# A fused block and two hybrid layers on one core: scaling of h spread later, h turned by VectorE and DRAM, V projected 512 columns at a time

## The reference

```
def hybrid_layer(x, norm_gain, w_in, w_out, rel_bias, cos, sin):
    hn = rms_norm_2(x, norm_gain)
    proj = hn @ w_in.astype(hn.dtype)
    cuts = list(np.cumsum(SPLIT_WIDTHS)[:-1])          
    aq, ak, av, ag, rq, rk, rv, rg = jnp.split(proj, cuts, axis=-1)
    ya = chunked_rel_attention(aq, ak, av, rel_bias)
    yr = chunkwise_retention(rq, rk, rv, cos, sin)
    y = jnp.concatenate([ya * jax.nn.silu(ag), yr * jax.nn.silu(rg)], axis=-1)
    return x + y @ w_out

def second_block(x, positions, norm_gain, w_in, w_out, rel_bias, final_gain):
    cos, sin = rotary_tables(positions, RET_HEAD_DIM)
    for layer in range(2):
        x = hybrid_layer(x, norm_gain[layer], w_in[layer], w_out[layer], rel_bias[layer], cos, sin)
    return rms_norm_2(x, final_gain)
```

## Time and profile before

| what | value |
|---|---|
| median of three runs | 1208.0 us (1207.38 to 1208.96) |
| profiled execution: time, span | 1208.31 us, 1206.5 us |
| TensorE (PE) busy, share of the span | 1192.2 us, 99% |
| VectorE (DVE) | 863.5 us, 72% |
| ScalarE (ACT) | 586.3 us, 49% |
| GpSimd (POOL) | 280.9 us, 23% |
| mean granted TensorE clock | 0.994 of full |

### The profile page before, as it was taken

One profiled execution on the slowest core, in us unless ns is written; L12 is line 12 of the kernel. 1 busy time (PEld: TensorE's weight loads), 2 busy tenths in 40 slices (PEclk: granted clock), 3 DMA queues, 4 the chain that ended last, 5 costly groups with the idle time before them and its releaser, 6 DMA issues.

```text
span 1206.5 us, 15740 instructions
## 1 busy us (share of the span) xinstructions
PE 1192.2 (99%) x5901; PEld 1012.0 (84%) x5901; DVE 863.5 (72%) x1425; ACT 586.3 (49%) x1048; POOL 280.9 (23%) x299
## 2 busy tenths in 40 slices
PE   8999999999999999999999989999999999999998
PEld 7888888888888888888888879899888889899886
DVE  6789655556786578537776798887747788986746
ACT  6666432324343344324435576854445577764442
...
GB/s 188 137 71 70 97 88 101 92 101 91 132 83 69 137 105 89 69 128 99 99 93 93 100 183 168 197 169 70 76 66 107 99 217 200 177 138 70 77 71 70
DMA packets 207697, 135.33 MB, mean 112 GB/s; under 512 B 5418, under 2 KB 200452, under 8 KB 207492
## 3 DMA queue, kind: packets, MB, share of 16 engines
...
## 4 chain that ended last, share of the span: by engine, by line
PE 93%; DVE 3%; ACT 1%; issue 1%; DMA 1%; SPq 0%; DVEq 0%; ACTq 0%
PE ps L191 92%; PE ps L194 1%; DVE b_sets L164 1%; DVE wlo L164 1%; DMA xtm<-in_x_dram 1%; ACT whi L161 0%; DMA raw<-in_w_in_dram 0%; ACT b_p L161 0%; DVE tmp L164 0%; DVE xtm L178 0%; ACT x1l L161 0%; DVE b_p L178 0%; SPq L197 0%; DVE b_pd L182 0%; ACT h L161 0%
## 5 line engine op out<-in xcount | busy, mean ns | idle before, releaser
L161 ACT ACTIVATE whi<-raw 128x1024 fp32r<-128x1024 f32 (+1 forms) x198 | 206.6, 1051 | 305.3 <-PE ps L191 294.5
L164 DVE TENSOR_TENSOR wlo<-raw,whi 128x1024 fp32r<-128x1024 f32 (+1 forms) x192 | 245.0, 1282 | 48.8 <-ACT whi L161 48.2
L191 PE MATMUL ps<-x0h,whi 128*128 128x512 f32 x1008 | 256.1, 392 | 0.0
L191 PE MATMUL ps<-x0l,whi 128*128 128x512 f32 x1008 | 255.5, 392 | 0.0
L191 PE MATMUL ps<-x0h,wlo 128*128 128x512 f32 x1008 | 254.0, 390 | 0.0
L191 PEld LDWEIGHTS ps<-x0h,wlo 128*128 128x128 f32 x1008 | 188.3, 188 | 38.8
L191 PEld LDWEIGHTS ps<-x0h,whi 128*128 128x128 f32 x1008 | 188.4, 189 | 38.2
L191 PEld LDWEIGHTS ps<-x0l,whi 128*128 128x128 f32 x1008 | 187.5, 188 | 38.0
L164 POOL TENSOR_TENSOR sums<-sums,sq 128x512 f32<-128x512 f32 x28 | 43.6, 1568 | 423.3 <-ACT sq L161 423.3
L191 PE MATMUL ps<-x1h,wlo 128*128 128x512 f32 x304 | 82.3, 389 | 0.0
L191 PE MATMUL ps<-x1h,whi 128*128 128x512 f32 x304 | 82.3, 389 | 0.0
(11 more groups left out here) (191 smaller groups left out, 1694.8 us busy)
## 6 DMA issues: line engine op xcount, KB each, us to landing
raw<-in_w_in_dram SPq DMA_DIRECT2D x98, 512.0 KB, 4.1
raw<-in_w_up_dram SPq DMA_DIRECT2D x44, 512.0 KB, 3.8
raw<-in_w_out_dram SPq DMA_DIRECT2D x24, 512.0 KB, 4.1
...
raw<-in_w_down_dram SPq DMA_DIRECT2D x16, 512.0 KB, 4.1
...
```

The lines of the kernel that those rows point to most:

```text
L161: return AC.put(lambda e: e.activation(o, i, func, **kw), after, AC, 1)
L164: return on.put(lambda e: e.tensor_tensor(o, a, b, op), after, on, 1)
L191: return PE.put(lambda e: e.matmul(o, l, r, start=start, stop=stop), after, PE if mark else None, 1)
```

## The change

The scaling of `H` in the first layer is taken out of `norm_steps` and becomes eight `h_final(k)`, begun at steps 49, 52, ... 70 of `layer_b(0)`, still on POOL. `h_turn(k)` no longer uses TensorE: VectorE turns the 32x32 blocks of a piece into `b_pd`, a DMA writes them to DRAM, and four `h_back(i)` DMAs read them back into `H`, tokens on the partitions, in another order of the columns, which the last additions follow through views of 32 columns. `project_v` is called twice a layer: 512 columns of V, 96 matmuls of 512 columns into four banks, one hook for each, weight tiles of two k by 512 columns, split one by one. The order of the projections, the steps of the heads and of the retention, and the inside of `ret` change with it: the third score comes one step earlier, the split takes two pieces instead of three and ends a step earlier, and `rsqrt_of` is on VectorE instead of POOL.

```diff
-            order = [4, 0, "v", 12, 5, 1, 13, 6, 2, "v", 14, 7, 3, 15]
-            order += [20, 16, "v", 21, 17, "v", 22, 18, 28, 23, 19, 29, 30, 31]
-            v_cols = iter([1024, 1280, 3072, 3328])
+            order = [4, 0, 5, "v", 1, 12, 6, 2, 13, 7, 3, 14, 15]
+            order += [20, 16, 21, "v", 17, 22, 18, 28, 23, 19, 29, 30, 31]
+            v_cols = iter([1024, 3072])
             for m in order:
                 if m == "v":
                     c0 = next(v_cols)
-                    plan_tm(wi2, 0, c0, 4, 256)
-                    plan_tm(wi2, 4, c0, 4, 256)
+                    for k0 in range(0, 8, 2):
+                        plan_tm(wi2, k0, c0, 2, 512)
...
-                    t2 = spread(RB2[:, :], r[:, 0:16], t)
-                    for k in range(8):
-                        t = tt(Hk(k), Hk(k), RB2[:, :], ALU.mult, after=[t2, h_read[k]], on=PO)
-                        h_tok[k] = ts(Hk(k), Hk(k), FIN(k), None, ALU.mult, after=t, on=PO)
-                    rb2_free.append(t)
+                    rb["rb2"] = spread(RB2[:, :], r[:, 0:16], t)
...
+        turn_free, h_back_tok = [[], []], []
+        HT = nc.dram_tensor("h_turned", (1024, 512), F32).ap()
...
-                ws, bs = [W.take() for _ in range(2)], [banks.next() for _ in range(2)]
-                free = [[], (), [v_read.get(s) for s in (0, 1)], [q_read.get(s) for s in (2, 3)]][j]
+                bs = [banks.next(), banks.next(), 5 + j, banks.next()]
+                frees = [[], []] if j == 0 else [[v_read[s] for s in (0, 1)], [q_read[s] for s in (2, 3)]]
                 r, tr_ = st["r"]
...
+                def evac(t, tok):
+
+                    bank, parts = bs[t], []
+                    for half in range(2):
+                        v = v_at(2 * j + half, t)
+                        if j == 0:
                             v = v.rearrange("p s (e c) -> p (s e) c", c=128)
-                        parts.append((v[:, :, 0:n], v[:, :, n:2 * n], src.rearrange("p (h c) -> p h c", c=n), r[:, t:t + 1]))
-                    for hi, _, src, rt in parts:
-                        th = act(hi, src, scale=rt, after=[tok, tr_, free])
+                        src = PS[bank][:, 256 * half:256 * half + 256].rearrange("p (h c) -> p h c", c=n)
+                        parts.append((half, v[:, :, 0:n], v[:, :, n:2 * n], src))
+                    th = [act(hi, src, scale=r[:, t:t + 1], after=[tok, tr_, frees[half]]) for half, hi, _, src in parts]
                     yield 1
...
+                    tl = [stt(lo, src, r[:, t:t + 1], f32(hi), ALU.mult, ALU.subtract, after=[tok, tr_, th, frees[half]])
+                          for half, hi, lo, src in parts]
                     bank_free[bank] = [th, tl]
...
+                    for half in range(2):
+                        tok_v.setdefault(2 * j + half, []).extend([th[half], tl[half]])
+
+                for kb in range(4):
+                    i, wh, wl = W.take()
+                    for t in range(4):
+                        for kk in range(2):
+                            k = 2 * kb + kk
+                            xh, xl = (x[:, k, 128 * t:128 * t + 128] for x in (X0.hi, X0.lo))
+                            first, end = k == 0, k == 7
+                            mm(PS[bs[t]][:, :], xh, wh[:, kk, :], first, False,
+                               after=[X0.th[k], W.hi[i], claim(bs[t]) if first else ()])
+                            hook()
+                            mm(PS[bs[t]][:, :], xh, wl[:, kk, :], False, False, after=[W.lo[i]])
+                            hook()
+                            tok = mm(PS[bs[t]][:, :], xl, wh[:, kk, :], False, end, after=[X0.tl[k]],
+                                     mark=end or (kk == 1 and t == 3))
+                            hook()
+                        if kb == 3:
+                            begin(evac(t, tok))
+                    W.done[i] = tok
+                    begin(W.split())
...
+            def h_final(k):
+
+                t = tt(Hk(k), Hk(k), RB2[:, :], ALU.mult, after=[rb["rb2"], h_read[k]], on=PO)
+                h_tok[k] = ts(Hk(k), Hk(k), FIN(k), None, ALU.mult, after=t, on=PO)
+                slot_free[5].append(t)
+                yield
+
...
+                o2, tp2 = score(2, 5, 0, claim(5))
                 yield 1
                 kp, pb, pfree = rps.take()
                 t0 = decay(0, o0, tp0)
...
                 t1 = decay(1, o1, tp3)
                 t3 = decay(3, o3, tp3)
                 bank_free[4] = [t3]
-                o2, tp2 = score(2, 5, 0, claim(5))
+                t2 = decay(2, o2, tp2)
+                bank_free[5] = [t2]
                 yield 1
                 _, pt, tfree = ptbs.take()
                 hi, lo = pt[:, 0:1280], pt[:, 1280:2560]
-                t2 = decay(2, o2, tp2)
-                bank_free[5] = [t2]
-                th = [act(hi[:, 0:512], pb[:, 0:512], after=[t0, tfree]),
-                      act(hi[:, 512:1024], pb[:, 512:1024], after=[t3, tfree])]
-                yield 1
-                th.append(act(hi[:, 1024:1280], pb[:, 1024:1280], after=[t2, tfree]))
+                cuts = ((0, 512), (512, 1280))
+                th = [act(hi[:, a:b], pb[:, a:b], after=[(t0, t2)[j], tfree]) for j, (a, b) in enumerate(cuts)]
+                yield 1
                 tl = [tt(lo[:, a:b], pb[:, a:b], f32(hi[:, a:b]), ALU.subtract, after=[th[j], tfree])
-                      for j, (a, b) in enumerate(((0, 512), (512, 1024)))]
-                yield 1
-                tl.append(tt(lo[:, 1024:1280], pb[:, 1024:1280], f32(hi[:, 1024:1280]), ALU.subtract, after=[th[2], tfree]))
+                      for j, (a, b) in enumerate(cuts)]
...
-                rr, t4 = rsqrt_of(sc, 4, 1.0 / 128, 1e-6, t3, on=PO)
+                rr, t4 = rsqrt_of(sc, 4, 1.0 / 128, 1e-6, t3)
...
-                free = claim(6)
-                for t in range(4):
-                    tp = tr(PS[6][:, 128 * t:128 * t + 128], H[:, 512 * k + 128 * t:512 * k + 128 * t + 128], IDENT,
-                            after=[h_tok[k], free], mark=t == 3)
-                yield 1
-                h_tok[k] = act(Hk(k), PS[6][:, :], after=[tp, h_read[k]])
-                bank_free[6] = [h_tok[k]]
-
+                pd = PD[:, 512 * (k % 2):512 * (k % 2) + 512]
+                t = blocks(pd.rearrange("p (i t c) -> p i t c", i=4, t=4),
+                           Hk(k).rearrange("p (t i c) -> p i t c", t=4, i=4), after=[h_tok[k], pd_free[0], turn_free[k % 2]])
+                turn_free[k % 2] = [dma(HT[128 * k:128 * k + 128, :], pd, d_ht[k % 2], after=t)]
+                h_read[k].append(t)
+                yield
+
+            def h_back(i):
+
+                src = HT.rearrange("(x j) (i c) -> i j x c", x=32, i=4)[i]
+                h_back_tok.append(dma(H[32 * i:32 * i + 32, :].rearrange("p (x c) -> p x c", c=128), src, d_hb,
+                                      after=[turn_free, [h_read[k] for k in range(8)]]))
+                yield
 
             start = step_no[0]
             at_step = lambda n, work: agenda.setdefault(start + n, []).append(work)
-            at_step(13 - l, head(0, 1))
-            for i in range(1, 8):
-                at_step(13 - l + 6 * i if i == 0 else 12 + 6 * i, head(i))
-            evs = []
-            for s in range(4):
-                evs += [ev_k(s), ev_q(s)] + [s // 2] * (s % 2 == 0) + [ev_g(s)]
-            for s in range(4, 8):
-                evs += [ev_r(s, "kh", "kl", rk_tok), ev_r(s, "qh", "ql", rq_tok)]
-                evs += [[2], [3], [ev_g(4)], [ev_g(5), ev_g(6), ev_g(7)]][s - 4]
-            for i, n in enumerate((66, 74, 82, 91)):
+            for i, n in enumerate((13 - l, 20, 27, 32, 37, 42, 48, 54)):
+                at_step(n, head(i))
+            att = [(ev_k, 0), (ev_q, 0), (ev_k, 1), 0, (ev_q, 1), (ev_g, 0), (ev_k, 2), (ev_q, 2), (ev_g, 1), (ev_k, 3), (ev_q, 3),
+                   (ev_g, 2), (ev_g, 3)]
+            rk = lambda s: ev_r(s, "kh", "kl", rk_tok)
+            rq = lambda s: ev_r(s, "qh", "ql", rq_tok)
+            att += [(rk, 4), (rq, 4), (rk, 5), 1, (rq, 5), (rk, 6), (rq, 6), (ev_g, 4), (rk, 7), (rq, 7), (ev_g, 5), (ev_g, 6),
+                    (ev_g, 7)]
+            evs = [e if isinstance(e, int) else e[0](e[1]) for e in att]
+            for i, n in enumerate((67, 76, 84, 92)):
                 at_step(n - 1, a_step_later(ret(i)))
-            if l == 1:
-                for k, n in enumerate((64, 66, 68, 74, 76, 78, 80, 85)):
-                    at_step(n, h_turn(k))
+            if l == 0:
+                for k in range(8):
+                    at_step(49 + 3 * k, h_final(k))
+            else:
+                for k in range(8):
+                    at_step(63 + 2 * k, h_turn(k))
+                for i in range(4):
+                    at_step(81 + 2 * i, h_back(i))
...
-        hv = H[:, :].rearrange("p (k t c) -> p k t c", k=8, c=128)
+        hv = H[:, :].rearrange("p (x t c) -> p x t c", t=4, c=32)
```

(1 more changed line is left out.)

43 lines of the change are left out of this document (7 added, 36 removed).

## The result

| | before | changed |
|---|---|---|
| median | 1208.0 us | 1214.96 us (1211.8 to 1215.6, five runs) |
| ratio | | 1.0052, 95% interval 1.0038 to 1.0065 |
| profiled execution: span | 1206.5 us | 1212.4 us |
| mean granted clock | 0.994 | 0.994 |

The account below looks back on a forecast made before the run. TensorE, busy 99% of the span, was taken as the bound. Terms -15.1 + 2.7 + 1.5 + 4.0 = -6.9 us gave 1201.4 us profiled, 1201.0 as median; range 1195 to 1207.

Parts of the forecast that it names:

- the waits that had a price in the forecast (8.2): New TensorE waits at bank 2 in layer 0's V, `ret(0)`'s V products and `ret(1)`'s scores: +2.7, +1.5 and +4.0 us.
- -5.0 (V): V projection: 384 matmuls of 512 columns replace pairs of 256 columns, saving 13 ns each, -5.0 us.
- -3.5 (turns): Turns of `H`: eight sets of four transposes leave TensorE, -3.5 us; their replacement costs nothing except in chains.
- Bank 2 in the first V call: TensorE waits for VectorE's evacuation of `ev_k(1)` to free the fourth bank: +2.7 us in layer 0, nothing in layer 1.
- a rival with 20%: The clock falls once or twice at a new wait, 3.0 us each: 1204 to 1207 us; chance 20%.
- `ret(1)`'s scores: At step 76 TensorE waits for the chain ending in VectorE's low part: +1.7 us in layer 0, +2.3 in layer 1.
- `ret(0)`'s V: Products with V wait behind VectorE's tiles and `b_pt`'s low part: 0.4 us in layer 0, 1.1 in layer 1, +1.5 together.
- The step that failed: Other moved heads finding `b_sets` or `b_pt` late was left uncosted, with slack claimed over 2 us in row order.
- the changed inside of `ret`: The rest of `ret`, two pieces instead of three and one step earlier, moves only low parts with slack; no cost.
- The -6.6: At `head(2)` of `layer_b(0)`, spreading the scaling of `H` removes the 3.6 us wait and 3.0 us of lower clock: -6.6 us.
- The rival on the slower side: Lower clock follows three of four new waits, 3.0 us each, and the waits stay: +2.1 us, 1210.1 and up; chance 8%.

Follow-up runs that it names:

- f5: Changed kernel with all but V's part undone, except that `ret` keeps its earlier third score and two pieces: 1210.93 us, ratio 1.0024.
- f2: Kernel before with only the turns of `H` moved to VectorE and DRAM: 1204.52 us, ratio 0.9972.
- g1: Changed kernel with bank 7 in place of bank 2 as fourth bank of each layer's first V call: 1209.56 us, ratio 1.0013.
- e3: Changed kernel with the eleven small `stat` rows of the retention norm on POOL again: 1211.06 us, ratio 1.0027.
- f1: Kernel before with only the scaling of `H` moved to steps 49 to 70: 1203.55 us, ratio 0.9963.
- e1: Changed kernel with the scaling of `H` back at the start of the first layer: 1211.88 us, ratio 1.0033.
- e2: Changed kernel with seven of the eight pieces of `H` left unscaled in the first layer: 1211.17 us, ratio 1.0030.
- f3: Changed kernel without its V part (V in quarters of 256 columns, with the order and heads' steps of before): 1200.95 us, ratio 0.9942.
- g5: Changed kernel with banks 7 and 5 as V's fourth, `head(6)`'s and `ret(1)`'s products with V one step later, norm's small rows on POOL: 1199.90 us.

## Why the prediction was wrong

By profiled executions the forecast was -6.9 us and the measured difference 1214.18 - 1208.31 = +5.9, so 12.8 are to be explained. From start to start, the waits that had a price in the forecast (8.2) took 6.5. Waits without a price took 8.6: 1.5 and 0.9 at bank 2 in the second V call, 2.6 and 1.4 at `head(6)`, 1.1 twice at `ret(1)`'s products. The lower clock took 3.8, small waits 1.7, and the saved work fell short by 0.4: 6.5 - 8.2 + 8.6 + 3.8 + 1.7 + 0.4 = 12.8.

**The work.** The terms -5.0 (V) and -3.5 (turns) were right: -4.8 in f5's trace, -3.7 in f2, -8.1 against -8.5 for both in the changed kernel. The matmul counts are those forecast, and eight V matmuls take 701.94 - 700.13 = 1.81 us:

```profile
700.13 0.39 PE L191 MATMUL ps<-whi,x0h 128*128 128x512 f32 x1
...
701.94 0.39 PE L191 MATMUL ps<-whi,x0l 128*128 128x512 f32 x1
```

The Trainium skill, "TensorE: Matmul & The Clock Gate", section "Back-to-back issue gap", gives 518 cycles for 512 columns, an estimated 0.216 us at 2.4 GHz, and by its figures V's term would have been an estimated 1.0 us. The runs disagree: 0.227 us from start to start, and 4.8 us of work saved in f5.

**Bank 2 in the first V call.** Mechanism and place were right, and so was the size: +2.7 forecast, 2.72 measured, none in layer 1. That it fits so closely is luck. TensorE was ready for the bank at about 690.3 and not 689.4, and VectorE's evacuation ended at 693.07 where 691.6 to 692.7 was reckoned; the two delays cancel:

```profile
684.96 0.65 DVE L164 TENSOR_TENSOR tmp<-ps,rb 128x512 f32<-128x512 f32 x1
...
688.09 4.27 DVE L164 TENSOR_TENSOR b_sets<-tmp,b_sets 64x512 fp32r<-64x512 f32 x6
...
692.38 0.69 DVE L164 TENSOR_TENSOR tmp<-ps,rb 128x512 f32<-128x512 f32 x1
```

What was left out of the sum is the clock behind it (4.6 us of excess in all); it stood as a rival with 20%. g1 shows that wait and clock go together.

**`ret(1)`'s scores.** +1.7 and +2.3 forecast, 1.04 and 1.64 measured; e3 shows the mechanism. **`ret(0)`'s V**, +1.5, was 0.5, in layer 1 alone.

**The step that failed** is the one that put the other heads at nothing: their slack was to be "over 2 us in the row order", and of the moved scaling the prediction says "The same slowing now meets heads 6 and 7 and the retention, where VectorE has idle time". No row of it shows that slack or that idle time. For `head(6)` the trace of the kernel before shows less: the low part of `b_pt` ends at 803.72 + 1.49 = 805.21, and TensorE needs it with the second of the eight matmuls, one distance of 0.23 us after 806.30:

```profile
803.72 1.49 DVE L164 TENSOR_TENSOR b_pt<-b_px,b_pt 128x1280 fp32r<-128x1280 f32 x1
...
806.30 1.40 PE L191 MATMUL ps<-b_pt,x1h 128*128 128x512 f32 x8
```

That is a slack of 1.3 us, and in `layer_b(1)` it is 1.3 as well (1065.89 to 1067.21). VectorE was busy 42.1 of the 50 us from 780 to 830, so by the average there was idle time; but a head's bias, softmax and turns, a rotary evacuation, a weight's low part and `b_pt`'s low part stand one behind the other just there. In the changed kernel `head(6)` waited 2.44 and 1.25 us. The second layer has no scaling, and f5, with the turns of `H` as before, waits 1.25 there too; so this wait comes of V's order and the heads' steps alone. In the first layer f1 (V as before) shows that the scaling alone used up the slack, with a wait of 0.85, and f5 (scaling as before) that V's order alone does so too, with 1.23. Undoing the scaling's move gives back 3.1 us of the median (e1) and leaving it out 3.8 (e2).

**A second omission** is of the same kind as the wait that was found. The count of 18 matmuls to the fourth bank was made for the first V call and not for the second, which leaves the same distance behind the rotary evacuation of s = 5: 1.32 and 0.71 us. `ret(1)`'s products (0.92 in each layer) had been set down with the changed inside of `ret`, as moving "only low parts with slack". f1 and f2, which have `ret` as before, wait no more than 0.30 us there, and f3, which has it changed, 0.92 and 0.99; in g5 both waits are gone.

**The -6.6** were not a term that V's new order would let stand beside its own, and they came from one execution. In f2's trace the same stall, 3.56 us, costs 5.5 with its clock in place of 6.7. f1 alone gives 4.7. In the changed kernel, undoing the spread (e1) brings nothing back at `head(2)`, and its 3.1 us come from the stretch near `head(6)`, less 2.1 that bank 2 takes: V's order and the spread both claimed the same stall.

**The rival on the slower side** named the clock behind three of the forecast waits. It had the right direction by a wrong road: the clock fell behind two waits, one of them not forecast, and cost some 1.7 and 2.1 us (4.6 less the 2.9 of the start-to-start gap; 7.4 less 1.5, 2.6 and 1.2). Plain waits at places without a price, 1.32 + 0.71 + 2.44 + 1.25 + 0.92 + 0.92 = 7.6 us of idle time by the rows above, weigh more.
